# Expert rows fetched from the first search on, ten up tiles per head, four activation buffers, gates in slabs of eight keys

## The reference

```python
q = (hc @ wq).reshape(PEER_BLOCK, PEER_HEADS, 2, PEER_DHALF)
sc = jnp.einsum('thcd,hckd->thck', q, keys)            # 8 heads, two halves, 128 keys each
s1, i1 = lax.top_k(sc[:, :, 0], 16)
s2, i2 = lax.top_k(sc[:, :, 1], 16)
cand = s1[..., :, None] + s2[..., None, :]             # 256 candidates a head
top, pos = lax.top_k(cand, 16)
gate = jax.nn.softmax(top)
act = gelu(einsum('thkd,td->thk', u_tab[eidx], hc))    # 128 experts a token, of 16384
out = einsum('thk,thkd->td', gate * act, v_tab[eidx])
```

## Time and profile before

| | |
|---|---|
| median of the runs | 5006.29 us (2 runs, 5004.76 to 5007.82) |
| the profiled execution | 4996.5 us, its span 4994.8 us |
| granted TensorE clock, mean | 0.897 of full speed |
| PE busy | 4135.7 us (83%) |
| DVE busy | 3209.8 us (64%) |
| ACT busy | 1390.2 us (28%) |
| POOL busy | 826.6 us (17%) |
| moved by DMA | 892.45 MB, mean 179 GB/s |

### The profile page before, as it was taken

One profiled execution on the slowest core, in us unless ns is written; L12 is line 12 of the kernel. 1 busy time (PEld: TensorE's weight loads), 2 busy tenths in 40 slices (PEclk: granted clock), 3 DMA queues, 4 the chain that ended last, 5 costly groups with the idle time before them and its releaser, 6 DMA issues. The chain is left out here.

```text
span 4994.8 us, 62496 instructions
## 1 busy us (share of the span) xinstructions
PE 4135.7 (83%) x24554; PEld 3746.9 (75%) x24554; DVE 3209.8 (64%) x5552; ACT 1390.2 (28%) x2133; POOL 826.6 (17%) x572
## 2 busy tenths in 40 slices
PE   6697767789999978888889776777999997887877
PEld 4477755469999978787776665555999996787876
DVE  7355444348879857666675554434887995666766
ACT  3430102233333422222233110223333342222222
POOL 2000000000002253344320000000000215334432
PEclk8898878899999988888889887888999999998988
DMA  5710021125456798888861001212545679888985
GB/s 181 249 64 1 1 96 49 51 83 153 147 179 240 285 342 304 289 291 285 293 211 64 1 1 61 84 51 72 152 147 176 224 287 355 299 293 295 313 280 201
DMA packets 371130, 892.45 MB, mean 179 GB/s; under 512 B 30208, under 2 KB 210560, under 8 KB 363680
## 3 DMA queue, kind: packets, MB, share of 16 engines
q1 hardware_dynamic: 297120, 620.14, 37.2%
q0 software_dynamic: 73728, 268.47, 14.8%
HBM read 755.32 MB, written 133.17 MB: 178 GB/s over the span
## 5 line engine op out<-in xcount | busy, mean ns | idle before, releaser
L200 PE MATMUL peer_ps<-gate_high,tile_high 128*128 128x384 f32 x2048 | 740.2, 361 | 259.2 <-DVE tile_low L193 259.1
L200 PE MATMUL peer_ps<-peer_h_high,tile_high 128*128 128x384 f32 (+1 forms) x2304 | 800.0, 347 | 78.0 <-ACT up_act L2037 58.6
L193 DVE TENSOR_TENSOR tile_low<-tile,tile_high 128x1024 fp32r<-128x1024 f32 x544 | 663.0, 1222 | 220.4 <-ACT tile_high L188 217.2
L201 PE MATMUL peer_ps<-peer_h_low,tile_high 128*128 128x384 f32 (+1 forms) x2304 | 790.5, 343 | 0.0
L202 PE MATMUL peer_ps<-peer_h_high,tile_low 128*128 128x384 f32 (+1 forms) x2304 | 789.8, 343 | 0.0
L1920 POOL DMA_INDIRECT row<-in_peer_u_rows,row_at x256 | 379.2, 1481 | 2280.7 <-DVE row_at L2225 1513.4
L201 PE MATMUL peer_ps<-gate_low,tile_high 128*128 128x384 f32 x2048 | 727.1, 355 | 0.0
L202 PE MATMUL peer_ps<-gate_high,tile_low 128*128 128x384 f32 x2048 | 724.8, 354 | 0.0
L200 PEld LDWEIGHTS peer_ps<-gate_high,tile_high 128*128 128x128 f32 x2048 | 419.2, 205 | 284.6 <-DVE tile_low L193 284.2
L188 ACT ACTIVATE tile_high<-tile 128x1024 fp32r<-128x1024 f32 x544 | 571.2, 1050 | 0.4 <-DMA tile<-in_peer_wq 0.4
L200 PEld LDWEIGHTS peer_ps<-peer_h_high,tile_high 128*128 128x128 f32 x2304 | 437.0, 190 | 102.6 <-issue 84.3
(11 more groups left out here) (405 smaller groups left out, 6160.0 us busy)
## 6 DMA issues: line engine op xcount, KB each, us to landing
tile<-in_peer_u SPq DMA_DIRECT2D x256, 512.0 KB, 4.0
tile<-in_peer_v SPq DMA_DIRECT2D x256, 512.0 KB, 6.2
acts<-up_act SPq DMA_DIRECT2D x256, 192.0 KB, 4.2
gates<-gates_out SPq DMA_DIRECT2D x24, 2048.0 KB, 9.3
gates_in<-gates SPq DMA_DIRECT2D x64, 768.0 KB, 11.5
act_in<-acts SPq DMA_DIRECT2D x256, 192.0 KB, 7.0
in_w<-in_w_in SPq DMA_DIRECT2D x36, 512.0 KB, 3.5
tile<-in_peer_wq SPq DMA_DIRECT2D x32, 512.0 KB, 3.9
```

Source lines behind the costliest of these rows:

```text
L193: return dve.tensor_tensor(out, value, high.bitcast(F32), ALU.subtract)
L200: pe.matmul(out, wh, mh, start=first, stop=False)
L201: pe.matmul(out, wh, ml, start=False, stop=False)
```

## The change

Six things:

1. `UPS_HEAD` 8 to 10, and `UPS_GROUP` gives 2 tiles in every third group and else 1, so that the search has 80 up tiles, the bridge 6, the groups 32 and the tail 10. DVE makes the two further low parts of a head at the end of its search.
2. The row addresses are computed per head, at the end of its search (two small operations on 128 x 16), and POOL waits for head n // 16 before each sixteenth fetch instead of for all.
3. `rows(...)` is moved up, and from the second head on DVE takes six dots in each search (`ROWS_BY_HEAD`), one after each of six of its parts: 42 by its end; two more before and two after the routes are turned. With one in each group and 2.5 for each tile of the tail, 95 dots are taken before the down stage (72 before the change). The other 33 go with the first 24 down tiles (`DOTS_UNTIL`), the adds with the last 102.
4. Four buffers `act_in` for two (`NACT`): SP issues `load_act(e)` when `weigh(e - 4)` is done.
5. Slabs of eight keys in two buffers, for four keys in three; slab s + 2 is issued when slab s has been used.
6. SP's order in the down stage: activations of e + 2, then tile e, then a slab if one is due.

```diff
-UPS_HEAD, UPS_BRIDGE = 8, 6
+UPS_HEAD, UPS_BRIDGE = 10, 6
-ROWS_BY_GROUP, ROWS_BY_TILE = 1, 2.3
-DOTS_UNTIL = 38
+ROWS_BY_HEAD, ROWS_BY_GROUP, ROWS_BY_TILE = 6, 1, 2.5
+DOTS_UNTIL = 24
-SLAB, NSLAB = 4, 3
+SLAB, NSLAB, NACT = 8, 2, 4
-UPS_GROUP = lambda g: 1 + g % 2
+UPS_GROUP = lambda g: 1 + (g % 3 == 0)
...
             def load_act(e):
-                if e >= 2:
-                    sp.wait_ge(weighed.sem, weighed.at(e - 1))
+                if e >= NACT:
+                    sp.wait_ge(weighed.sem, weighed.at(e - NACT + 1))
                 sp.wait_ge(act_stored[e % 2].sem, act_stored[e % 2].at(16 * (e // 2 + 1)))
-                sp.dma_start(acts_in[e % 2][:, :], acts[e]).then_inc(act_loaded[e % 2].sem, 16)
+                sp.dma_start(acts_in[e % NACT][:, :], acts[e]).then_inc(act_loaded[e % NACT].sem, 16)
...
-                        load_act(0)
-                        load_act(1)
+                        for e in range(NACT):
+                            load_act(e)
...
-            for e in range(2, NKEY):
-                load_act(e)
-                if e + 1 < NKEY:
-                    load(UPS + e + 1)
-                if e % SLAB == SLAB - 2 and e // SLAB + 2 < SLABS:
-                    load_slab(e // SLAB + 2)
+            for e in range(NRAW, NKEY):
+                if e + 2 < NKEY:
+                    if e == NRAW:
+                        load_act(e + 1)
+                    load_act(e + 2)
+                load(UPS + e)
+                s = (e - NRAW) // SLAB + NSLAB
+                if (e - NRAW) % SLAB == SLAB - 1 and s < SLABS:
+                    load_slab(s)
 
         @block.gpsimd
         def _(pool):
-            pool.wait_ge(found.sem, found.at(1))
             for n in range(2 * ROWS):
+                if n < ROWS and n % TOPK == 0:
+                    pool.wait_ge(rows_found.sem, rows_found.at(n // TOPK + 1))
...
+            def some_rows(hd, site):
+                if hd:
+                    rows((hd - 1) * ROWS_BY_HEAD + site)
...
                 link(last)
+                link(dve.scalar_tensor_tensor(out=row_atf[:, :], in0=chosen[:, TB - 1, 1, own], scalar=float(NKEY),
+                                              in1=chosen[:, TB - 1, 0, own], op0=ALU.mult, op1=ALU.add))
+                dve.tensor_scalar(row_at[:, own], row_atf[:, :], float(layer * NKEY * NKEY), None, ALU.add).then_inc(rows_found.sem, 1)
                 lows(1)
+                some_rows(hd, 6)
...
+            last.then_inc(found.sem, 1)
             lows(1)
+            searched_rows = rows_done[0]
+            rows(searched_rows + 2)
             dve.wait_ge(flip_taken.sem, flip_taken.at(TB - 1))
             lows(2)
+            rows(searched_rows + 4)
...
                 lows(UPS_GROUP(g))
-                rows(ROWS_BY_GROUP * (g + 1))
+                rows(searched_rows + 4 + ROWS_BY_GROUP * (g + 1))
             for m in range(done[0], UPS):
                 lows(1)
-                rows(ROWS_BY_GROUP * GROUPS + int(ROWS_BY_TILE * (m - GROUP_AT[GROUPS])))
+                rows(searched_rows + 4 + ROWS_BY_GROUP * GROUPS + int(ROWS_BY_TILE * (m + 1 - GROUP_AT[GROUPS])))
```

More of the change, by code:

```diff
@@ L1794, in peer @@
     summed, taken = pg.counts("tile_summed"), pg.counts("tile_taken")
-    act_stored, act_loaded = ([pg.counts(f"act_{n}{b}") for b in range(2)] for n in ("stored", "loaded"))
+    act_stored = [pg.counts(f"act_stored{b}") for b in range(2)]
+    act_loaded = [pg.counts(f"act_loaded{b}") for b in range(NACT)]
+    rows_found = pg.counts("rows_found")
     gates_stored = [pg.counts(f"gates_stored{b}") for b in range(2)]
@@ L1847, in peer @@
         slabs = [buf(f"gates_in{b}", [P, TD // SPILL, SLAB * SPILL]) for b in range(NSLAB)]
-        acts_in, mixed = ([buf(f"{n}{b}", [P, TD]) for b in range(2)] for n in ("act_in", "weighed"))
+        acts_in, mixed = ([buf(f"{n}{b}", [P, TD]) for b in range(count)] for n, count in (("act_in", NACT), ("weighed", 2)))
         gh, gl = ([buf(f"gate_{n}{b}", [P, TD], F32R) for b in range(NSPLIT)] for n in ("high", "low"))
@@ L2139, in _, with rows @@
             ramp = across(pg.c["ramp"][:, 0:TOPK])
+            rows_done = [0]
+            def rows(until):
+                for n in range(rows_done[0], until):
+                    dve.wait_ge(row_loaded[n % NROW].sem, row_loaded[n % NROW].at(16 * (n // NROW + 1)))
+                    x, j = row[n % NROW][:, :], n % ROWS
+                    if n == 0:
+                        dve.wait_ge(h_flipped.sem, h_flipped.at(2))
+                    if n < ROWS:
+                        last = dve.scalar_tensor_tensor(out=x, in0=x, scalar=1.0, in1=h_own[:, :], op0=ALU.mult, op1=ALU.mult,
+                                                        accum_out=dots[:, j:j + 1])
+                    elif j == 0:
+                        last = dve.tensor_scalar(own_sum[:, :], x, dots[:, 0:1], None, ALU.mult)
+                    else:
+                        dve.wait_ge(row_used.sem, row_used.at(n))
+                        last = dve.scalar_tensor_tensor(out=own_sum[:, :], in0=x, scalar=dots[:, j:j + 1], in1=own_sum[:, :],
+                                                        op0=ALU.mult, op1=ALU.add)
+                    last.then_inc(row_used.sem, 1)
+                    rows_done[0] = n + 1
+            def some_rows(hd, site):
+                if hd:
+                    rows((hd - 1) * ROWS_BY_HEAD + site)
             def search(hd):
@@ L2147, in search @@
                     lows(1)
+                    some_rows(hd, two_tb + 1)
                 dve.sem_inc(searched.sem, 1)
@@ L2156, in search @@
                 lows(1)
+                some_rows(hd, 3)
                 dve.tensor_scalar(spot[0][:, :, :], pos[:, :, :], 4, None, ALU.logical_shift_right)
@@ L2166, in search @@
                 lows(1)
+                some_rows(hd, 4)
                 for j in range(2):
@@ L2171, in search @@
                 lows(1)
+                some_rows(hd, 5)
                 for j in range(2):
@@ L2260, in weigh @@
                 s = e // SLAB
-                dve.wait_ge(act_loaded[e % 2].sem, act_loaded[e % 2].at(16 * (e // 2 + 1)))
+                dve.wait_ge(act_loaded[e % NACT].sem, act_loaded[e % NACT].at(16 * (e // NACT + 1)))
                 dve.wait_ge(slab_loaded[s % NSLAB].sem, slab_loaded[s % NSLAB].at(16 * (s // NSLAB + 1)))
                 by = lambda x: x.rearrange("p (g t) -> p g t", t=SPILL)
-                dve.tensor_tensor(by(mixed[e % 2][:, :]), by(acts_in[e % 2][:, :]),
+                dve.tensor_tensor(by(mixed[e % 2][:, :]), by(acts_in[e % NACT][:, :]),
                                   slabs[s % NSLAB][:, :, (e % SLAB) * SPILL:(e % SLAB + 1) * SPILL], ALU.mult).then_inc(weighed.sem, 1)
@@ L2302, in peer @@
         s.passed(n)
+    rows_found.passed(PH)
+    for b in range(NACT):
+        act_loaded[b].passed(16 * NKEY // NACT)
     for b in range(2):
-        for s in (act_stored[b], act_loaded[b]):
-            s.passed(16 * NKEY // 2)
+        act_stored[b].passed(16 * NKEY // 2)
         gates_stored[b].passed(16 * TD // SPILL // 2)
```

1 line of the change is left out of this document (added).

## The result

The changed kernel takes 5199.81 us (median of 2 runs, 5198.14 to 5201.48) against 5006.29: a ratio of 1.0387, 95% interval 1.0342 to 1.0431. It is slower by 3.9%, where 4730 was predicted. The profiled execution has a span of 5199.6 us, and PE's mean granted clock is 0.888 (0.897 before), while every engine's busy time is within a few us of what it was, but for POOL's: PE 4142.3 us, DVE 3214.0, ACT 1390.0, POOL 781.8. So no work was added; somewhere the engines stand. The table by stage, layer 1, says where.

A forecast was written before the change was run, and what follows sets the result against it. It saw the largest loss in the down stage's waits for activations, with DMA the next bound there. 4996.5 + 2 x (-1 - 138) = 4718.5, plus 9.8 to the median: 4728, stated as 4730; 8-in-10 range 4645 to 4860.

The forecast's parts named there:

- DVE takes over: 24 x 9.39 = 225: Groups: PE loses four tiles, so DVE sets the pace at 9.39 us a group, 225 us, -10 us.
- C: Down stage: v tile behind a slab lands 27 us or more after issue; slower than before, 5110 us; chance 0.04.
- +66.7 us predicted: Search: sixteen more up tiles at 4.17 us of PE each, with DVE staying under PE, +66.7 us a layer.
- rival D: Search: dots wait for row fetches, so DVE becomes the bound; +10 us a head, 4800 us; chance 0.04.
- 79 predicted: Tail: ten transfer-bound tiles at 5.6 us plus a stall of 23 make 79 us, -60 us a layer.
- moving tiles into the search: Up stage: it only takes out idle PE time that the larger stall gives back, -1 us a layer.
- covers 7.2 and 11.5 us: Down stage: four buffers issue activation loads over 8 us earlier, enough for activation (7.2 us) and slab (11.5 us) landing times.
- 582 predicted: Down stage: 4.55 us a tile, 582 us, -138 us a layer.
- DMA becomes the bound, just above PE: Down stage: transfers at a share of 0.95 to 0.97 take 4.5 to 4.6 us a tile, against PE's 4.17.
- A: Down stage: v tile behind the 1.5 MB slab is late; 4.8 to 5.3 us a tile, 4857 us; chance 0.22.
- rival B: Down stage: packets overlap better, so PE is the bound at 4.2 to 4.3 us a tile; 4652 us; chance 0.17.
- a slab that lands 2 us later than 11.5: Down stage: with queues served packet by packet, the doubled slab lands only some 2 us later; by bytes up to 23.

The follow-up runs named there:

- lead2: The changed kernel with low parts made up to BRIDGE + 3 instead of BRIDGE + 1, two tiles ahead when the groups begin: 4759.47 us, ratio 0.9497.
- Experiment 9: lead2 with eight up tiles a head, the old groups of 1 and 2, and 1.14 rows a tail tile: 4732.55 us, ratio 0.9446.
- experiment 6: The kernel before with four `act_in` buffers and nothing else changed: 4676.86 us, ratio 0.9333.
- lead2_slab4: lead2 with slabs of four keys in three buffers again: 4656.41 us, ratio 0.9296.
- lows_first: The changed kernel, lead still zero, with each group's low parts made ahead of the next group's one-hots: 4824.88 us, ratio 0.9647.

## Why the prediction was wrong

**The step that failed** is "DVE takes over: 24 x 9.39 = 225" for the groups. It added up DVE's busy time per group, and a sum of busy times is the length only if DVE never waits. Whether it waits depends on the order in DVE's queue and on how many low parts are in hand, and the earlier trace rows show only a group that has that lead. The diff showed the rest: 16 more tiles ahead of the groups, and a `lows` line whose argument had been negative. The section on the change even said that the two further low parts of a head are made "at the end of its search", and the count was not carried on to tile 102. The stage missed by 223 us in each layer, 447 us together; the profiled time (5201.5) lies 483 above the sum (4718.5), and the rest is in the bridges, the tails and the down stages, below. (lead2's expectation still puts layer 2 at 457 us, from a window that began 21 us before its first one-hot.) None of the rivals was this one: C ended at slower than before, but in the down stage.

**The rest of the sum held, partly for a wrong reason.**
- Search: +66.7 us predicted, 424.5 - 358.5 = 66.0 measured, PE full and DVE at 0.90. The prediction read 344.9 us for DVE in the search before; in the earlier trace rows that is PE's weight loads, and DVE has 314.2. No term used it, since the sum took DVE's side from the earlier trace rows. DVE never waited there for a row; rival D did not come. POOL's 48 fetches beside it took 47.9 us, one each. (DVE's waits for rows are 17.6 us in the whole kernel, 9.3 of them in layer 1's tail.)
- Bridge: +2.3 predicted, 33 us against 25.
- Tail: 79 predicted, 88 and 89.5 measured. The stall that was set at 23 is there, 23.6:

```profile
PE peer_ps L200 <- ACT up_act L2044: 25.6, 2, 23.6
```

- Up stage as a whole: moving tiles into the search was put at about nothing. Experiment 9 says 27 us worse over both layers.
- Activations: "covers 7.2 and 11.5 us" held. DVE's 213 us of waits for `act_in` are gone, and experiment 6 shows that this one part is worth 334 us by itself (5010.6, the kernel before beside it, to 4676.9).
- Down stage: 582 predicted, 593 and 590.5 measured, and "DMA becomes the bound, just above PE" was wrong. The share was 0.91, not 0.95, and the waits were those named as the sign of A:

```profile
ACT gate_high L188 <- DMA tile<-in_peer_v: 212.8, 55, 11.3
...
PE peer_ps L200 <- DVE tile_low L193: 35.9, 14, 5.9
```

The total of the first row is not the sign: ACT runs ahead and waits for tiles anyway, 209.2 us in 72 times in lead2_slab4, where PE is full. The longest is, 11.3 us against 7.0 there. And PE's waits for the low part are 14, as many as the slabs that were loaded in this window (2110 to 2680). The size came out near by luck: A came, at 4.6 us a tile, below the 4.8 to 5.3 that it was given, and so next to the 4.55 of another mechanism. The assumption that failed is that two queues' packet times add up to at most one: experiments 6 and 7 reach 1.04 and 1.02. That was rival B, and it is what the stage does when the slabs are small.

The prediction weighed a rule of the Trainium skill (DMA: Bandwidth & Descriptors, Queues, rings and completion order), by which engines go round between queues by packet, and drew from it a slab that lands 2 us later than 11.5; by bytes it was 23. In lead2 the median slab landed in 16.2 us, between them. The prediction's "the trace agrees" says too much: in the earlier trace rows q1 passed 1470 of the profile's packets and q0 751, so they do not take turns one for one. And the rule did not bear on what cost the time: the tile stands behind the slab in the *same* queue.

**What the change is worth in its parts.** Against 5006: four `act_in` buffers alone 4677; all six parts with the lead restored 4759; with small slabs 4656; with eight tiles a head besides 4634. The change as made has one part that surely pays (334 us), the early rows and what goes with them, which together pay 32 to 43, one part that takes back 103 us, one that takes back 27, and a lead lost on the way that costs 440.

**What stays open:** the last 27 to 35 us between the split slab and the small one; why late rows cost 72 us with large slabs, and which of parts 2, 3 and 6 pays with small ones; and which of the small waits of lows_first make its 65 us over lead2.

## What to carry to other kernels

In a pipeline of engines with queues in order, count at each boundary of stages how many items the producer has in hand, before and after a change of the tile counts, and check that every filler line still reaches as far as the old constants did; the busy time per turn is the length of a turn only with that lead. The sign in this profile was a pair of waits of almost equal count (22 and 23), A for B and B for A, with no engine busy for more than 0.6 of the time. And when a transfer is enlarged, ask what stands behind it in the same queue: its bytes at once can be too much where its bytes per time are no problem.

## What the runs showed of the hardware

- The profile's share of the DMA engines is no ceiling at 1. With two queues busy it was 1.04 over 545 us at 379 GB/s, and 1.02 over 520 us at 371 GB/s.
- The Trainium skill (Perfetto Trace Analysis, DMA Optimizations) holds larger transfers to be better for bandwidth, and says that splitting may help where DMA engines are generally idle. Here splitting a 1.5 MB transfer gained 76 us in a stage whose share was 0.94: what counted was not the bandwidth but when the next transfer of that queue lands.
- A gap of 8 us in PE's work costs more than itself. With one such gap in every 18.75 us, the granted clock of the stage was 0.79, and each tile took 7.0 us where it takes 4.2 with PE full.
